# HGRN2 decay levels: one schedule step per level split into exponents, operands, product and select

## What is computed

```python
q = silu(q_raw) * DK ** -0.5
f = lb + (1.0 - lb) * sigmoid(z);  log_f = log(maximum(f, LOG_FLOOR))
k = (1.0 - lb) * sigmoid(-z)
b = cumsum(log_f)                                  # along the tokens
attn[t, s] = sum_d q[t, d] * k[s, d] * exp(b[t, d] - b[s, d])   # s <= t
o = rmsnorm(attn @ v + (q * exp(b)) @ S, onorm_g)  # S: state of the chunks before
y_a = o * silu(gate)
```

## Time and profile before

| | us |
|---|---|
| median of 3 runs (1398.03 to 1400.15) | 1399.65 |
| the profiled execution | 1402.71 |
| its span, first to last instruction | 1400.9 |
| TensorE busy in it | 1314.9 |
| VectorE, ScalarE, GpSimd busy in it | 724.0, 639.0, 585.4 |
| layer 0: HGRN2 items and their levels | about 60 to 260 |
| layer 1: the same | about 738 to 940 |

### The profile page before, as it was taken

The page is one execution under the profiler, slowest core; times in us unless marked ns, Lnnn a source line. Parts: engine busy times, 40 slices in busy tenths (PEclk is TensorE's granted clock), DMA queues, the critical chain, the costliest instruction groups (busy, mean ns, idle before and its releaser), DMA issues.

```text
span 1400.9 us, 16591 instructions
## 1 busy us (share of the span) xinstructions
PE 1314.9 (94%) x5920; PEld 1042.4 (74%) x5920; DVE 724.0 (52%) x1163; ACT 639.0 (46%) x987; POOL 585.4 (42%) x751
## 2 busy tenths in 40 slices
PE   3989999999999999999979988999999999999996
PEld 2877777787777777788857776778877777778885
DVE  6777775624555424444257787652255441443333
ACT  3355554543555344445335555454355433444531
POOL 3243333554232535454525433344523243454451
PEclk9999999999999999999989999999999999999998
DMA  9321112333222323333312211223311222222321
GB/s 360 110 83 47 61 61 68 120 126 122 83 69 96 130 91 108 103 120 104 100 68 91 76 45 46 75 76 120 116 58 59 85 91 83 90 80 86 100 97 60
DMA packets 40785, 131.82 MB, mean 94 GB/s; under 512 B 5248, under 2 KB 5376, under 8 KB 39424
## 3 DMA queue, kind: packets, MB, share of 16 engines
q1 hardware_dynamic: 30336, 111.57, 23.3%
q10 hardware_dynamic: 10368, 19.21, 4.5%
HBM read 128.13 MB, written 2.10 MB: 93 GB/s over the span
## 4 chain that ended last, share of the span: by engine, by line
PE 78%; DVE 11%; ACT 6%; issue 3%; DMA 1%; ACTq 0%; DVEq 0%
PE ps_st L757 20%; PE ps_st L759 20%; PE ps_st L758 20%; PE ps_o L779 4%; PE ps_s L853 2%; PE ps_s L808 1%; PE ps_s L877 1%; PE ps_w L862 1%; PE ps_misc L774 1%; DVE hg_x L1400 1%; ACT w_hi L931 1%; ACT gate_t L955 1%; DVE hg_at L1432 1%; DVE gate_x L1250 1%; DVE cq_raw L1609 1%
## 5 line engine op out<-in xcount | busy, mean ns | idle before, releaser
L640 POOL TENSOR_TENSOR w_lo<-raw,w_hi 128x256 fp32r<-128x256 f32 x736 | 574.6, 813 | 774.7 <-ACT w_hi L931 774.7
L757 PE MATMUL ps_st<-h_hi,w_hi 128*128 128x512 f32 x984 | 404.9, 411 | 0.2 <-POOL w_lo L640 0.2
L759 PE MATMUL ps_st<-h_hi,w_lo 128*128 128x512 f32 x984 | 386.7, 393 | 0.0
L758 PE MATMUL ps_st<-h_lo,w_hi 128*128 128x512 f32 x984 | 386.0, 392 | 0.0
L757 PEld LDWEIGHTS ps_st<-h_hi,w_hi 128*128 128x128 f32 x984 | 187.0, 190 | 46.1 <-issue 6.6
L758 PEld LDWEIGHTS ps_st<-h_lo,w_hi 128*128 128x128 f32 x984 | 186.9, 190 | 43.1 <-issue 6.5
L759 PEld LDWEIGHTS ps_st<-h_hi,w_lo 128*128 128x128 f32 x984 | 186.2, 189 | 40.4
L931 ACT ACTIVATE w_hi<-raw 128x1024 fp32r<-128x1024 f32 x184 | 193.2, 1051 | 29.4 <-PE ps_st L759 26.2
L953 ACT ACTIVATE gate_t<-gate_x 128x512 f32<-128x512 f32 x80 | 50.5, 632 | 248.2 <-DVE gate_x L1250 248.2
L1250 DVE TENSOR_SCALAR gate_x<-ps_st 128x512 f32<-128x512 f32 x79 | 54.5, 690 | 203.5 <-PE ps_st L759 203.2
L808 PE MATMUL ps_s<-hg_x 128*128 128x128 f32 x384 | 51.8, 282 | 21.0 <-DVE hg_x L1400 20.9
(11 more groups left out here) (277 smaller groups left out, 2024.4 us busy)
## 6 DMA issues: line engine op xcount, KB each, us to landing
raw<-w_stream SPq DMA_DIRECT2D x184, 512.0 KB, 3.4
mod_w<-w_mod ACTq DMA_DIRECT2D x64, 256.0 KB, 2.7
pro_w<-w_mod_first SPq DMA_DIRECT2D x8, 1024.0 KB, 13.9
x<-x_t SPq DMA_DIRECT2D x4, 512.0 KB, 7.8
ret_decay<-decay ACTq DMA_DIRECT2D x2, 1024.0 KB, 6.1
out_t<-o_t SPq DMA_DIRECT2D x8, 256.0 KB, 2.2
raw_extra<-w_stream SPq DMA_DIRECT2D x2, 512.0 KB, 20.0
cs<-cst SPq DMA_DIRECT2D x1, 836.0 KB, 8.8
```

Source lines behind the costliest of these rows:

```text
L640: ins = nc.gpsimd.tensor_tensor(lo[:, r], whole[:, r], hi[:, r].bitcast(F32), ALU.subtract)
L757: nc.tensor.matmul(dst[0:m, :], wh, hi, start=(k == 0), stop=False)
L758: nc.tensor.matmul(dst[0:m, :], wh, lo, start=False, stop=False)
L759: last = nc.tensor.matmul(dst[0:m, :], wl, hi, start=False, stop=(k == nk - 1))
```

## The change

The step "hg_lv" is replaced by steps "ex" (exponents), "xb" (operands), "mm" (product) and "sel" (select) with the level as third field. "ex", "xb" and "sel" are in `EARLY`; "mm" is TensorE's alone. In the groups of head h (b = h - 1 is the head before) they stand so, and `mixers_first` and the banks follow:

```diff
-        return ([("hg_lv", h - 1, 4), ("hg_lv", h - 1, 5)],
-                [("hg_lv", h - 1, 6), ("hg_lv", h - 1, 7), ("hz", h, 1), ("hz", h, 2), ("hg_cross", h - 1)],
-                [("hz", h, 3), ("hg_pv", h - 1), ("hg_lv", h, 0), ("hg_lv", h, 1), ("hg_out", h - 1)],
-                [("hg_v", h), ("hg_lv", h, 2), ("hg_lv", h, 3)])
+        b = h - 1
+        return ([("sel", b, 0), ("sel", b, 1), ("xb", b, 2), ("xb", b, 3), ("ex", b, 4), ("mm", b, 2), ("mm", b, 3), ("hg_pv", h - 2)],
+                [("hz", h, 1), ("sel", b, 2), ("sel", b, 3), ("xb", b, 4), ("hz", h, 2), ("ex", b, 5), ("mm", b, 4),
+                 ("hg_out", h - 2)],
+                [("sel", b, 4), ("xb", b, 5), ("ex", b, 6), ("hz", h, 3), ("ex", h, 0), ("ex", h, 1), ("mm", b, 5)],
+                [("sel", b, 5), ("xb", b, 6), ("xb", h, 0), ("xb", h, 1), ("ex", h, 2), ("ex", h, 3), ("mm", b, 6), ("hg_cross", b),
+                 ("hg_v", h), ("mm", h, 0), ("mm", h, 1)])
...
-                  ("cq", 1): [("hg_v", 0), ("hg_lv", 0, 0), ("hg_lv", 0, 1)], ("cq", 2): [("hg_lv", 0, 2), ("hg_lv", 0, 3)]}
+        head_0 = {("q", 0): [("hz", 0, 1)], ("i", 0): [("hz", 0, 2)], ("cq", 1): [("hz", 0, 3), ("ex", 0, 0), ("ex", 0, 1)],
+                  ("cq", 2): [("xb", 0, 0), ("xb", 0, 1), ("ex", 0, 2), ("ex", 0, 3), ("hg_v", 0), ("mm", 0, 0), ("mm", 0, 1)]}
...
-    item("cq", 5)
-    s += [("hg_pv", h - 1)]
+    tail = [[t for t in steps if t[0] != "hz" and t[1] < h] for steps in hg_first(h)]
+    for j in range(3):
+        item("cq", 3 + j)
+        s += tail[j]
     item("ckv", 0)
-    s.append(("cq_norm",))
+    s += tail[3] + [("cq_norm",)]
     item("ckv", 1)
-    s += [("hg_out", h - 1), ("cq_rest",)]
+    s += [("hg_pv", h - 1), ("cq_rest",)]
     item("kr", 0)
-    s.append(("ckv_norm",))
+    s.append(("hg_out", h - 1))
     ma = merge_items("a")
     item(*ma[0])
-    s.append(("kr_rope",))
+    s += [("ckv_norm",), ("kr_rope",)]
...
         elif kind == "hg_v":
-            use("w0", s)
+            use("o", s)
...
+        hg_e6 = at("hg_e6", 86 * KB + KB // 2, [P, 2, 3 * P])
...
-                    before = 7 * h + (6 if n == 6 else max(n - 1, 0))
-                    if before:
+                    before = 7 * h + (-1, -1, 1, 2, 3, 4, 0)[n]
+                    if before > 0:
                         dve.wait_ge(x_built, e.at(x_built, before))
```

More of the change, by code:

```diff
@@ L141, in build_schedule @@
             item(kind, h)
-            s += [t for t in steps if t not in begun]
+            s += [t for t in steps if t[1] >= 0 and t not in begun]
     h = HG_HEADS
[L144 to L147, removed]
-    item("cq", 5)
-    s += [("hg_pv", h - 1)]
+    tail = [[t for t in steps if t[0] != "hz" and t[1] < h] for steps in hg_first(h)]
+    for j in range(3):
+        item("cq", 3 + j)
+        s += tail[j]
     item("ckv", 0)
-    s.append(("cq_norm",))
+    s += tail[3] + [("cq_norm",)]
     item("ckv", 1)
-    s += [("hg_out", h - 1), ("cq_rest",)]
+    s += [("hg_pv", h - 1), ("cq_rest",)]
     item("kr", 0)
-    s.append(("ckv_norm",))
+    s.append(("hg_out", h - 1))
     ma = merge_items("a")
     item(*ma[0])
-    s.append(("kr_rope",))
+    s += [("ckv_norm",), ("kr_rope",)]
     for it in ma[1:-3]:
@@ L244, in build_uses @@
                 out += 1
[L245 to L250, removed]
+        elif kind == "mm" and s[2] < 6:
+            use(("s0", "s1")[s[2] % 2], ("lv", s[1], s[2]))
+        elif kind == "mm":
+            use("w0", ("cross0", s[1]))
+            use("w1", ("cross1", s[1]))
         elif kind in ("hg_pv", "ret_pv"):
@@ L306 @@
 USES, BANK_USES = zip(*[build_uses(layer) for layer in range(DEPTH)])
-EARLY = ("hz", "hg_lv", "mod_acc")
+EARLY = ("hz", "sel", "xb", "ex", "mod_acc")
 LATER = ("hg_v", "hg_out", "mla_pv", "ret_out")
@@ L800, in _ @@
                         transposes(s, lambda k: hg_vt[:, k * P:(k + 1) * P])
-                    elif kind == "hg_lv" and 1 <= s[2] <= 6:
-                        h, n = s[1], s[2] - 1
+                    elif kind == "mm" and s[2] < 6:
+                        h, n = s[1:]
                         pe.wait_ge(x_built, e.at(x_built, 7 * h + n + 1))
@@ L809, in _ @@
                         done(last, ("lv", h, n))
-                    elif kind == "hg_lv" and s[2] == 7:
+                    elif kind == "mm":
                         h = s[1]
@@ L829, in _ @@
                         pe.wait_ge(o_sq_ready, e.at(o_sq_ready, (0 if kind == "hg_out" else HG_HEADS) + s[1] + 1))
-                        column_sums(s, o_sq[:])
+                        column_sums(s, (t2 if kind == "hg_out" else o_sq)[:])
                     elif kind in ("cq_norm", "ckv_norm"):
@@ L1086, in _ @@
                         copy_out(s, hg_v[:, s[1] % 2, :, :].rearrange("p a b -> p (a b)"))
-                    elif kind == "hg_lv":
+                    elif kind == "ex":
                         h, n = s[1:]
-                        if n <= 6:
-                            act.wait_ge(d_ready, e.at(d_ready, 7 * h + n + 1))
+                        act.wait_ge(d_ready, e.at(d_ready, 7 * h + n + 1))
                         if n < 5:
@@ L1117, in _ @@
                         src = bank[e.bank_of(s)]
-                        A(o_sq[:], src[:], ACT.Square).then_inc(o_sq_ready, 1)
+                        A((t2 if kind == "hg_pv" else o_sq)[:], src[:], ACT.Square).then_inc(o_sq_ready, 1)
                     elif kind in ("hg_out", "ret_out"):
@@ L1570, in _ @@
                         hz(*s[1:])
[L1571 to L1583, removed]
+                    elif kind == "ex":
+                        level_exponents(*s[1:])
+                    elif kind == "xb":
+                        level_operands(*s[1:])
+                    elif kind == "sel":
+                        level_select(*s[1:])
                     elif kind in ("hg_out", "ret_out"):
```

16 lines of the change are left out of this document (7 added, 9 removed), and 3 rows, old and new, of the table head_0.

## The result

| | before | changed |
|---|---|---|
| median of 4 runs each, on the same chip | 1399.74 us (1398.03 to 1400.15) | 1388.99 us (1386.04 to 1389.62) |
| ratio, with its 95% interval | | 0.992 (0.9908 to 0.9932) |
| span of the profiled execution | 1400.9 us | 1384.2 us |

What follows compares the result with a forecast made beforehand. TensorE, busy 94% of the span, was taken as the bound. Of 44.7 us (34.6 of waits, 10.1 of clock drops) 20.8 would be left, a gain of 23.9 us, giving 1375.7 us; range 1360 to 1393.

Steps and rivals of the forecast that it cites:

- The long term: Cross products of heads 2 and 3 in each layer: 3.1 us wait plus 1.7 us clock drop, 4 times 4.8 us.
- In head 1 it is not [...] no wait: Head 1's cross product, without hg_out in its group: operands 6 at 12.0 us, TensorE at 12.7, no wait.
- about 0.3 us each: Tail cross products, with hg_out but no running sum or next head: about 0.3 us of wait, counted twice.
- the 1 us of the first head: Level products of layer 0's first head: between 0 and 2.4 us left of 4.77 us; 1 us taken.
- My margin: Head 1's cross product: operands 6 ready at 12.0 us and TensorE there at 12.7, a margin of 0.7 us.
- rival C: Chain too long in head 1 and the tail too: four more 2 us waits, 1384 to 1393 us; chance 0.18.
- So 4.5 us and two drops go: ckv_norm's column sum, moved behind one more item: its 4.5 us wait for ScalarE's root and two clock drops vanish.
- rival E: Freed time is waited for again on weights: 1399 us; chance 0.05.
- three of four at 0.88: VectorE's halves of levels 0 and 1: three at 0.88 us beside GpSimd, one at 0.34, done at 7.7 us.
- strict turns: VectorE and GpSimd alternating on the shared port: 1.1 us a half, four 4.5 us; sum 6 us slower than forecast.
- B: No wait is left, GpSimd's bursts falling beside the halves and the root coming earlier: 1355 to 1361 us; chance 0.11.
- D: VectorE's queue bounds every round and hg_pv waits for bank o: 18 us slower, 1418 us; chance 0.11.

Runs made afterwards that it cites:

- e2: Changed kernel with hg_out's column sum and reciprocal root one step earlier, right behind the gate q: 1363.82 us, ratio 0.9736 to the kernel before.
- e9: e2 with the early root put behind the rounding of the weights on ScalarE: 1367.44 us, ratio 0.9777 to the kernel before.
- e5: Changed kernel with operands 6 moved one group earlier, ahead of hg_out, the product for q and select 5: 1365.93 us, ratio 0.9757 to the kernel before.
- e4: Changed kernel with GpSimd's subtraction replaced by a memset, leaving out the weights' low parts: 1351.01 us, ratio 0.9643 to the kernel before.
- e1: Kernel before with only the tail of the change (ckv_norm's sums one item later): 1401.92 us, ratio 1.0008 to the kernel before.
- e10: Changed kernel, operands 6 ahead of hg_out, root early, hg_out's VectorE part later, turned values through bank misc, ckv_norm's root behind the rounding: 1358.86 us, ratio 0.9707.
- e8: e1 with ckv_norm's root on ScalarE behind the rounding of the merge item's weights: 1394.47 us, ratio 0.9960 to the kernel before.

## Why the prediction was wrong in size

**The long term was right.** The walk of heads 2 and 3 gave operands 6 at 16.7 us from the end of item q and TensorE at 13.6. Found: item q ends near 137.55; operands 6 are done at 154.8, so at 17.3, and TensorE is there at 13.56. The wait is 3.75 instead of 3.1, because the fourth half was slow too and its exponential, and with it the root, came later. The drop behind it was rightly counted. The experiments show that the mechanism is this one: e2 and e9 take the wait for the root out of that chain, e5 all that stood between the halves and operands 6, e4 the collisions; in each the wait shrinks or goes, and the drop goes with it.

**The step that failed is the part that I took as nothing: "In head 1 it is not [...] no wait", the tail's "about 0.3 us each", and the 1 us of the first head.** They came to 3.6 + 3.2 + 3.7 = 10.5 us instead of 1.6, which is 8.9 of the 13.6 us by which the list above ends higher (34.4 for 20.8); 2.6 more are the long term, 2.1 the merge items, priced at nothing too. For head 1 I let VectorE begin select 4 at 1.0 us after item q, as in the later rounds. TensorE's product 4 and VectorE's timeline of the changed kernel:

```profile
104.06 1.16 PE L811 MATMUL ps_s<-hg_x 128*128 128x128 f32 x8 [0.76 <-DVE hg_x L1402]
```

```profile
105.86 0.69 DVE L1373 SCALAR_TENSOR_TENSOR hg_e<-centre,hg_b 128x512 f32<-128x512 f32 x1
...
107.19 0.15 DVE L1433 COPY carry<-cs 128x1 f32<-128x1 f32 x1
...
113.85 1.23 DVE L1264 SCALAR_TENSOR_TENSOR hg_q<-gate_x,gate_t 128x512 f32<-128x512 f32 x1
...
117.83 0.97 DVE L1417 TENSOR_TENSOR hg_kd<-hg_e,hg_k 128x384 f32<-128x384 f32 x1
```

Product 4 started at 104.06, so VectorE is 3.1 us behind it at select 4 (107.19) and still busy with the exponents of level 5 till then: it comes late out of the first head's levels. That is 2.1 us more, and the product for q took 1.23 beside GpSimd, where I had 0.7. My margin was 0.7; 2.1 + 0.5 - 0.7 = 1.9, and the wait is 1.81. What makes VectorE late is GpSimd's work: the operands of levels 0 and 1 of the first head (84.76 to 88.24) run beside a burst at 0.77 to 0.88 each, and the level products wait from there on. In e4 select 4 stands 1.4 us behind product 4 (104.48 for 103.12), and neither the level products nor head 1's cross product wait. For the tail I made no walk at all; VectorE waits there 2.35 us for the root, with two slowed instructions of 1.24 and 1.10 us ahead of it:

```profile
220.11 0.75 DVE L1585 SCALAR_TENSOR_TENSOR y_t<-ps_o,cur,rstd 128x512 f32<-128x512 f32 x1 [2.35 <-ACT rstd L942]
...
226.94 0.97 DVE L1417 TENSOR_TENSOR hg_kd<-hg_e,hg_k 128x384 f32<-128x384 f32 x1
```

In e9, with the root early and the burst where it was, the tail doesn't wait.

Head 1 and the tail are rival C in its places (four more waits), with 6.8 us of waits and without drops. It had a chance of 0.18. That the time lies in its range as well (1384 to 1393 us) is in part luck: its four waits add 6.2 us to the forecast's 0.6 and would give 1382 by themselves; the level products, the merge items and the long term did the rest.

**`ckv_norm`.** "So 4.5 us and two drops go" held in the list of waits, but I did not ask what stands behind the moved step on ScalarE. In e1 that is worth the whole gain. In the change 2.1 us of waits were left of it: against e1, the column sum of the last head's output is 8.7 us earlier there (243.32 for 252.01), but the rounding of these weights 11.0 (256.65 for 267.65), so it is 2.3 us less late, and the wait behind it 0.88 us instead of 3.14. It is rival E's mechanism (time given back on weights) in one place.

**Halves beside GpSimd.** I took three of four at 0.88 and set the price by counting; the fourth half costs 0.5 us per round here, 2 us in the four rounds, but what the burst's start decides is larger (3.6 to 4.6 us between e2 and e9). By strict turns, as I read the Trainium skill ("SBUF — State Buffer", section "SBUF: two separate sides"), an estimate for the four is 4.5 us; they took 3.5 (142.12 to 145.63), so the trace does not agree with that size. It agrees with the section's condition that GpSimd's instruction must read SBUF: in e4 a half at 138.98 went at 0.34 while the memset ran from 138.35 to 139.43.

**Rivals B and D** are out: the cross waits stayed, and the weighted values waited nowhere for bank o. How far D was is shown by e10: the same instructions of VectorE in another order, and TensorE waits 6.0 us at level and cross products instead of 25.5.

Left open: how much of the 10.75 us the split of the levels gives without the tail's move; the change without that move was not tried, and what the move gave on the kernel before (nothing in e1, 5.9 us in e8) need not add up with it. Of the layers' stretches in the two profiled traces some 4 us more than the 10.3 are gained, of which shorter level products are 2 (their busy time fell by 0.8 and 1.2 us); the rest is not assigned.

## What to carry to other kernels

When a stage is taken apart so that each part waits an item less, look at what its last part now stands behind in each in-order queue: here one list entry (operands 6 ahead of the previous head's output) was worth some 22 us, twice the whole change. Walk the first, the second and the last round with their own start times; a round in steady state says little of them. And a step that is moved for TensorE's sake moves on ScalarE too: see which rounding it now stands ahead of, because that sets when weights are ready and when GpSimd's burst falls on VectorE.

## What was not expected of the hardware

An instruction with one SBUF tensor and a column of scalars as input was slowed beside GpSimd as much as those with two (the halves, 0.42 to 0.96 of busy time): the product of `hg_qc` with `g_last` (128x128) took 0.29 us in e5 with GpSimd idle (145.42) and 0.63 at 152.42 in the change with GpSimd at work. In e4 the one that ran wholly beside the memset took 0.50 (111.89), though the memset reads nothing; that is a single row. `y_t`, which reads PSUM, took 0.75 in both cases (143.64 in e2, beside GpSimd; 147.58 in the change, not).

A drop of the clock behind a wait is partly paid back by the next wait where VectorE sets the pace: in the kernel before, the 2.42 us at 179.02 with its drop of 1.7 were followed by a cross wait of 0.47 at 188.61; in e8 the same 2.42 us came without a drop, and the cross wait behind it was 2.03. Both sums are near 4.5 us.
